# A decoder trunk of two layers: the value products of the latent attention at full array width, one head of a pair at a time

## The reference

```python
kv = rms_norm(kv_lat, kv_norm_g) @ w_ukv
k_nope, v_a = kv[..., :MLA_NOPE], kv[..., MLA_NOPE:]
qa = jnp.concatenate([q_nope, q_pe], axis=-1)[:, :, None]
o_a = causal_block_attention(qa, ka, v_a, 1.0 / math.sqrt(MLA_NOPE + MLA_ROPE), lambda p: p[:, :, 0])
y_a = o_a.transpose(0, 2, 1, 3).reshape(bsz, s, MLA_HEADS * MLA_V) @ w_out_mla
...
merged = gates[:, :, 0] * y_a + gates[:, :, 1] * y_b + gates[:, :, 2] * y_c
return merged @ w_o
```

## Time and profile before

| | |
|---|---|
| median of 3 runs | 1044.84 us (1044.05 to 1045.74) |
| profiled execution | 1044.84 us, its span 1042.4 us |
| busy in the span | PE 987.3 us (95%), PEld 916.4 (88%), DVE 747.6 (72%), ACT 520.4 (50%) |
| mean granted TensorE clock | 0.978 |
| chain that ended last, by engine | PE 67%, DVE 16%, issue 11%, DMA 2% |
| HBM read | 199.83 MB, 193 GB/s over the span |

### The profile page before, as it was taken

How to read it: one execution, slowest core, us unless ns; L and a number is a source line. 1 busy time by engine, 2 the same in 40 slices (tenths; PEclk the granted TensorE clock), 3 DMA queues, 4 the chain that set the end, 5 groups by cost and what they waited for, 6 DMA issues and landing times.

```text
span 1042.4 us, 20388 instructions
## 1 busy us (share of the span) xinstructions
PE 987.3 (95%) x7817; PEld 916.4 (88%) x7817; DVE 747.6 (72%) x1119; ACT 520.4 (50%) x725; POOL 18.0 (2%) x23
## 2 busy tenths in 40 slices
PE   3599999989999999999999999998999999999997
PEld 2498899889898999989898999887998989999997
DVE  2438889996485787876345698999568578788733
ACT  2555355548434555654345544654743465555523
POOL 5000000000000000000000000000000000000001
PEclk8799999999999999999999999999999999999999
DMA  9865545536694455966763545535668635554551
GB/s 308 290 202 164 176 147 179 180 107 216 233 360 162 148 176 166 350 241 240 274 205 98 161 137 172 183 124 176 202 240 301 218 128 164 170 192 164 182 183 41
DMA packets 138951, 202.23 MB, mean 194 GB/s; under 512 B 3416, under 2 KB 114148, under 8 KB 138852
## 3 DMA queue, kind: packets, MB, share of 16 engines
q1 hardware_dynamic: 138501, 200.68, 57.4%
q10 hardware_dynamic: 351, 0.21, 0.1%
HBM read 199.83 MB, written 1.05 MB: 193 GB/s over the span
## 4 chain that ended last, share of the span: by engine, by line
PE 67%; DVE 16%; issue 11%; DMA 2%; SPq 2%; ACT 1%; DVEq 0%; ACTq 0%
PE PB L1279 15%; PE PB L1281 14%; PE PB L1280 14%; DVE wL L861 5%; DVE buf L950 4%; PE SC L1279 2%; PE SC L1280 2%; PE SC L1281 2%; PE MI L1230 2%; DMA raw<-in_w_in 2%; PE PB L1302 1%; DVE rdev L1008 1%; PE ST L1332 1%; DVE cb L1096 1%; PE PB L1303 1%
## 5 line engine op out<-in xcount | busy, mean ns | idle before, releaser
L861 DVE TENSOR_TENSOR wL<-raw,wH 128x2048 fp32r<-128x2048 f32 (+3 forms) x152 | 322.9, 2126 | 123.2 <-ACT wH L606 121.1
L1279 PE MATMUL PB<-hH,wH 128*128 128x256 f32 x1376 | 399.5, 290 | 11.8 <-DVE wL L861 11.7
L1280 PE MATMUL PB<-hL,wH 128*128 128x256 f32 x1376 | 391.9, 285 | 0.0
L1281 PE MATMUL PB<-hH,wL 128*128 128x256 f32 x1376 | 391.8, 285 | 0.0
L606 ACT ACTIVATE wH<-raw 128x2048 fp32r<-128x2048 f32 (+3 forms) x152 | 268.4, 1782 | 128.2 <-DMA raw<-in_w_down 58.4
L1279 PEld LDWEIGHTS PB<-hH,wH 128*128 128x128 f32 x1376 | 266.5, 194 | 27.0 <-issue 15.2
L1280 PEld LDWEIGHTS PB<-hL,wH 128*128 128x128 f32 x1376 | 266.8, 194 | 0.9 <-issue 0.7
L1281 PEld LDWEIGHTS PB<-hH,wL 128*128 128x128 f32 x1376 | 266.5, 194 | 0.0
L950 DVE SCALAR_TENSOR_TENSOR buf<-G,vec,buf 128x256 f32<-128x256 f32 x240 | 98.0, 477 | 0.3
L1302 PE MATMUL PB<-hH,wH 128*128 128x256 f32 x192 | 57.5, 300 | 15.1 <-DVE hL L878 12.2
L1096 DVE SCALAR_TENSOR_TENSOR cb<-PB,vec,cb 128x255 f32<-128x255 f32 (+1 forms) x88 | 36.3, 475 | 32.2 <-ACT cb L752 32.2
(11 more groups left out here) (257 smaller groups left out, 1694.1 us busy)
## 6 DMA issues: line engine op xcount, KB each, us to landing
raw<-in_w_in SPq DMA_DIRECT2D x48, 1024.0 KB, 5.4
raw<-in_w_up SPq DMA_DIRECT2D x44, 1024.0 KB, 5.1
ada<-in_ada_w SPq DMA_DIRECT2D x40, 1024.0 KB, 7.3
raw<-in_w_down SPq DMA_DIRECT2D x22, 1024.0 KB, 4.9
ada_pre<-in_ada_w SPq DMA_DIRECT2D x8, 1024.0 KB, 11.7
raw<-in_w_o SPq DMA_DIRECT2D x8, 1024.0 KB, 8.4
raw<-in_w_out_diff SPq DMA_DIRECT2D x4, 1024.0 KB, 5.2
raw<-in_w_out_conv SPq DMA_DIRECT2D x4, 1024.0 KB, 7.3
```

The source lines that it names most:

```text
L861: dve.tensor_tensor(wL[s][:, 0:size], raw[s][:, 0:size], wH[s][:, 0:size].bitcast(F32), ALU.subtract).then_inc(w_lo[s], 1)
L1279: pe.matmul(out, a, xh(k), start=first and k == 0, stop=False, skip_group_check=True)
L1280: pe.matmul(out, a, xl(k), start=False, stop=False, skip_group_check=True)
L1281: ins = pe.matmul(out, b, xh(k), start=False, stop=last and k == kt - 1, skip_group_check=True)
```

## The change

The value products of a pair are made as two uses of the bank `OB`, A and B. Each multiplies the full `vM` (the values of both heads, 128 columns) with one head's weights, and only the 64 partitions of that head are read. The A use comes in the step of the B transposes (19, 24, 29, 34), ahead of them; the B use stays where the product of the pair was (21, 26, 31, 35). ScalarE and VectorE then round and subtract 64 partitions in each of the eight steps. There is one buffer `PT` in place of two, and `E` and `vD` change places in `xn`.

```diff
-OB_USES = ["V0", "PD0", "V1", "PD1", "PD2", "PD3", "PM0", "PM1", "PM2", "PM3"]
+OB_USES = ["V0", "PD0", "V1", "PD1", "PD2", "PD3", "PM0A", "PM0B", "PM1A", "PM1B", "PM2A", "PM2B", "PM3A", "PM3B"]
...
-VALUES_AT = {9: "PD0", 11: "PD1", 14: "PD2", 16: "PD3", 21: "PM0", 26: "PM1", 31: "PM2", 35: "PM3"}
+VALUES_AT = {9: "PD0", 11: "PD1", 14: "PD2", 16: "PD3", 19: "PM0A", 21: "PM0B", 24: "PM1A", 26: "PM1B",
+             29: "PM2A", 31: "PM2B", 34: "PM3A", 35: "PM3B"}
...
-        E = flat_xn[:, 0:768].rearrange("p (m s) -> p m s", m=2)
-        vD = [flat_xn[:, 768 + i * 512:768 + (i + 1) * 512].rearrange("p (k t) -> p k t", k=2) for i in range(2)]
-        PT = [PT0, flat_xn[:, 1024:1024 + 384]]
+        vD = [flat_xn[:, i * 512:(i + 1) * 512].rearrange("p (k t) -> p k t", k=2) for i in range(2)]
+        E = flat_xn[:, 1024:1024 + 768].rearrange("p (m s) -> p m s", m=2)
...
-                        act.activation(oAH[:, int(use[2]), :], OB[:, 0:T], ACT.Copy).then_inc(o_hi, 1)
+                        p, r0 = int(use[2]), 0 if use[3] == "A" else 64
+                        act.activation(oAH[r0:r0 + 64, p, :], OB[r0:r0 + 64, 0:T], ACT.Copy).then_inc(o_hi, 1)
...
-                    act.activation(PT[TRANSPOSE_AT[n][3:] == "B"][:, :], TR[:, 0:384], ACT.Copy).then_inc(tr_read, 1)
+                    act.activation(PT[:, :], TR[:, 0:384], ACT.Copy).then_inc(tr_read, 1)
...
-                    p = int(use[2])
-                    dve.wait_ge(o_hi, l * 4 + p + 1)
-                    dve.tensor_tensor(oAL[:, p, :], OB[:, 0:T], oAH[:, p, :].bitcast(F32),
+                    p, r0 = int(use[2]), 0 if use[3] == "A" else 64
+                    dve.wait_ge(o_hi, l * 8 + 2 * p + (use[3] == "B") + 1)
+                    dve.tensor_tensor(oAL[r0:r0 + 64, p, :], OB[r0:r0 + 64, 0:T], oAH[r0:r0 + 64, p, :].bitcast(F32),
...
-                    before = "T" + use[1:] + ("B" if use[1] == "M" else "")
+                    before = "T" + use[1:]
...
-                        for t, (t0, at) in enumerate(((0, slice(0, T)), (P, slice(T, T + P)))):
-                            for m in range(2):
-                                r = slice(64 * m, 64 * m + 64)
-                                ins = pe.matmul(OB[r, t0:T], vM[int(use[2]) % 2][:, t, r], PT[m][:, at], start=(t == 0),
-                                                stop=(t == 1), tile_position=(0, 64 * m), skip_group_check=True)
-                        ins.then_inc(ob_full, 1)
+                        v = [vM[int(use[2]) % 2][:, t, :] for t in range(2)]
+                    pe.matmul(OB[:, 0:T], v[0], PT[:, 0:T], start=True, stop=False, skip_group_check=True)
+                    pe.matmul(OB[:, P:T], v[1], PT[:, T:T + P], start=False, stop=True,
+                              skip_group_check=True).then_inc(ob_full, 1)
```

More of the change, by code:

```diff
@@ L300, in trunk_kernel @@
         W = sb("W", [P, 2, 384], F32, heads)
-        PT0 = sb("PT0", [P, 384], F32, heads)
+        PT = sb("PT", [P, 384], F32, heads)
         heads.close()
@@ L1349, in attention @@
                         v = [vD[i][:, t, h * P:(h + 1) * P] for t in range(2)]
-                        pe.matmul(OB[:, 0:T], v[0], PT[0][:, 0:T], start=True, stop=False, skip_group_check=True)
-                        pe.matmul(OB[:, P:T], v[1], PT[0][:, T:T + P], start=False, stop=True,
-                                  skip_group_check=True).then_inc(ob_full, 1)
                     else:
```

## The result

The changed kernel takes 1051.22 us (median of 4 runs, 1051.03 to 1051.36) against 1044.77 of the kernel before: a ratio of 1.0063, 95% interval [1.0047, 1.0079], 6.45 us slower. The forecast was 1051.0.

> The changed kernel once more, beside the others of this set on one chip: 1051.2 us, as before.

A forecast was written before the change was run, and what follows sets the result against it. VectorE's taps pace steps 8 to 25, TensorE from there to step 35. Per layer 0.68 + 0.66 - 0.23 + 2.11 - 0.14 = 3.08, two layers 6.2 us, 1044.84 + 6.2 = 1051.0 us; range 1047.6 to 1054.6.

The forecast's parts named there:

- The wait of step 34: Before chunk 35: oAL of 3A stands ahead of both merges, +2.11 us a layer, 0.66 product and 1.45 waiting.
- the rival of a hidden wait: Step 34: ScalarE and VectorE turn the half round sooner, the 1.45 us goes twice, 1048.1 us; chance 0.11.
- the row-for-row chain of step 35: Product, oAH, oAL, merge, then TensorE again, as traced in step 35; its timings priced step 34's wait.
- TensorE in steps 29 and 31: Product 2A adds 0.66 us in full in step 29; step 31 gives back 0.23.
- the edge ahead of the scores: TensorE's gap on entering packed work, 0.21 us instead of 0.12, absent after the change.
- The 1.78 us for a pair: Alternative product price from the skill's up to 2x for two column tiles, each half 0.89 us; 0.66 was taken instead.
- Step 29's slack: The rotation of pair 3 ends 1.94 us later but has 0.86 us of slack before TensorE's scores, so hidden.
- The handover: From VectorE's taps to TensorE's layer norm sums: 0.34 us more VectorE in each of steps 19 and 24, +0.68 us.
- the gain of step 35: Step 35 keeps its chain of three engines, 0.14 us shorter.
- Cover: TensorE's own 0.66 us falls into its idle before chunk 21, and likewise before chunk 26; it costs nothing.
- The granted clock: Rival: the clock falls in step 34 after some 1.2 us idle, costing 2 x 1.7 us, 1054.4 us; chance 0.14.
- The rival that the filled wait keeps the clock up: Shorter idle before chunks 21 and 26 keeps 2.4 GHz, 6.8 us at most back, 1044.2 us; chance 0.05.

The follow-up runs named there:

- experiment 1: Changed kernel with the oAL of product 3A put behind the two merges of step 34 on VectorE: 1047.72 us, ratio 1.0035.
- experiment 4: Kernel before with full-width products, both in the old steps 21, 26, 31 and 35, and evictions in halves: 1049.89 us, ratio 1.0049.
- experiment 8: Changed kernel with every half product on a tile of 64 columns, one at a time, in the new steps: 1054.27 us, ratio 1.0090.
- Experiment 6: Changed kernel with two unused reciprocals added on VectorE in step 29, behind oAL: 1053.59 us, ratio 1.0085.
- Experiment 3: Kernel before, products still packed, with oAH and oAL each in two instructions of 64 partitions: 1047.25 us, ratio 1.0029.
- experiment 7: Changed kernel with the two heads of a pair in the other order, partitions 64 to 127 in the A step: 1052.64 us, ratio 1.0074.
- experiment 2: Kernel before with the oAL of step 35 put behind the two merges of that step: 1043.74 us, ratio 0.9989.
- experiment 5: Changed kernel with two unused reciprocals added on VectorE in step 24, behind oAL: 1056.97 us, ratio 1.0114.

## Why the prediction was right

**The wait of step 34.** The prediction had 2.11 us a layer and the trace has 2.08, of it 1.43 waiting, which experiment 1 took away by VectorE's order alone. So the rival of a hidden wait is out. The step was priced by carrying the row-for-row chain of step 35 over to step 34, and that chain proved exact to 0.03 us at each link.

**TensorE in steps 29 and 31.** The trace has +0.66 and -0.24, the prediction +0.66 and -0.23. The scores behind the product too run 0.10 us shorter: 0.45 us between their first rows, in place of 0.55. It is 0.44 behind the full-width products of experiment 4 and 0.55 behind the tiles of experiment 8, so this goes with the tile. I had counted only the edge ahead of the scores. The 1.78 us for a pair, worked out from the 2x, was not what came: experiment 8 shows that it is near the price of halves kept on tiles (0.79 each, and an edge of 0.09), not of halves at full width.

**Step 29's slack.** The prediction had 0.86 us, and in the trace of the changed kernel TensorE waits for nothing in step 31. Experiment 6 measured 0.88.

**The handover, mis-sized.** "So no wait, but 0.34 us of VectorE ... and the same in step 24: +0.68 us" was 1.01. There is no wait indeed, and oAL takes 0.34 in each of steps 19 and 24, but step 21's oAL, which I counted as unchanged, had become dearer: 0.12 in front, 0.12 behind and 0.12 behind the row maxima, though it moves half the data. Experiment 3 had the two behind (its handover +0.68 is 0.54 for the second half and 0.13 behind the row maxima), and experiment 7 moved them to the other steps. The one in front is explained only by the pattern of experiment 7, read from rows. The 0.12 behind oAL also ate the gain of step 35, -0.02 in place of -0.14. In the table's terms the forecast was short by 0.33 at the handover and by 0.12 in step 35, and over by 0.11 between the scores and chunk 34, by 0.03 in step 34 and by 0.01 in step 31: 3.08 + 0.45 - 0.15 = 3.38. By the traces the forecast was thus 0.6 us too low over both layers. That it lies within 0.2 us of the median is partly luck: the medians differ by 6.45 us, the traces by 6.81.

**Cover.** TensorE's 0.66 in step 19 went into chunk 21's wait, as said: 1.86 before, 1.20 after. The like wait before chunk 26 went from 2.58 to 1.91.

**Rivals.** The granted clock did not fall in step 34: after the idle of 1.19 us behind the three transposes it was 1.00 from 281 to 285 us. The rival that the filled wait keeps the clock up failed by its own condition, since VectorE sets the pace there (with 3.00 of 3.00 us busy in both rows below); and the clock was no matter of the wait's length alone. After 1.20 us of idle it fell in the first layer and held in the second, in one execution:

```profile
185.00:188.00 3.00, 2.73 (x13) 2.73 (x14) 3.00 (x9) 1.67 (x4) 0.00 (x0) 0.59 0.84 244
```

```profile
689.00:692.00 3.00, 2.86 (x24) 2.87 (x25) 3.00 (x9) 1.54 (x4) 0.00 (x0) 1.00 0.90 270
```

"That the clock stays up I hold for likely" was thus half wrong. It cost nothing, because chunk 21 is not on the path. Nor does the shorter idle explain where the clock stayed up: in experiment 2, with the idle unshortened at 1.86 us, the clock was 0.61 from 185 to 188 us in the first layer and 1.00 from 686 to 689 in the second. That it did not fall at the handover of the changed kernel either may be luck too. The prediction had no term for that, and in one layer of experiment 2 and in both of experiment 5 a fall there cost some 1.6 us a layer.

## What to carry to other kernels

When work is moved ahead in a hand-written order, look at what stands behind its eviction on the evicting engine: here four tenths of the loss, 1.43 of 3.38 us a layer, came from one small subtraction put in front of two merges that freed the banks. Price such a wait by the nearest place where the same chain already runs, link by link. And ask of each stage which engine paces it: the same 1.67 us of VectorE moved the work behind it by 0.8 us in one step and by 1.6 in another, where a lower clock took as much again.

## What the runs showed of the hardware

A float32 subtraction on VectorE of 64 partitions and 256 columns took 0.42 us, as one of 128 did, and on partitions 64 to 127 the next instruction started 0.12 us later than behind partitions 0 to 63; the rows fit a delay whenever VectorE changes the partitions at which it starts in a memory. ScalarE took 0.38 us for either. A value product on one tile of 64 columns held TensorE 0.79 us, on the full array 0.65, and two such tiles side by side 0.80. The same idle of 1.20 us was followed by a granted clock of 0.59 in one layer and 1.00 in the other.
